# Later layers' attention heads in pairs, keys by queries, weights summed by GpSimd

## The reference

```python
def window_gqa(q, k, v, kc, vc, sink):            # 4 heads, 2 of keys; |query - key| <= 128, + context, + sink
    p = softmax([s_loc, s_ctx, s_sink])
    return p_loc @ v_band + p_ctx @ vc
def diff_weights(q, k, v, lam):                   # 4 heads, two maps of width 32 each
    p = softmax(q @ k^T * 32 ** -0.5)
    return (p[:, :, 0] - lam * p[:, :, 1]) @ v    # keys: 512 tokens and 256 of context
def neighbourhood_attn(q, k, v, kc, vc, rpb):     # 4 heads, width 64; bias by relative row and column
    p = softmax([q @ k^T * 64 ** -0.5 + bias, q @ kc^T * 64 ** -0.5])
    return p_loc @ v + p_ctx @ vc
def ctx_attn(q, k, v, sink=None):                 # layer 2 only: the context's own queries, 256 keys
```

## Time and profile before

| what | value |
|---|---|
| median of 3 runs | 3963.61 us (3963.18 to 3972.03) |
| profiled execution, its own time | 3965.11 us |
| its span | 3963.4 us |
| busy: TensorE, VectorE, ScalarE, GpSimd | 3588.4, 1845.8, 1207.2, 1069.6 us |
| mean granted TensorE clock | 0.937 of full speed |

### The profile page before, as it was taken

How to read it: one execution, slowest core, us unless ns; L and a number is a source line. 1 busy time by engine, 2 the same in 40 slices (tenths; PEclk the granted TensorE clock), 3 DMA queues, 4 the chain that set the end, 5 groups by cost and what they waited for, 6 DMA issues and landing times. The chain is left out here.

```text
span 3963.4 us, 46334 instructions
## 1 busy us (share of the span) xinstructions
PE 3588.4 (91%) x17668; PEld 2809.5 (71%) x17668; DVE 1845.8 (47%) x3445; ACT 1207.2 (30%) x1687; POOL 1069.6 (27%) x643
## 2 busy tenths in 40 slices
PE   6997999999687799999989878999999989879998
PEld 5864788878376678885666546888898467557887
DVE  5433433365444465653527773744355417652111
ACT  2253322233311332222015453222344014443222
POOL 2322434444344233441000003343401000024444
PEclk8998999999798899999989878999999998789999
DMA  5510344422000034441110001444454110002221
GB/s 221 203 54 18 121 161 163 154 87 100 26 1 1 30 115 156 160 152 55 54 53 1 1 1 53 154 145 176 147 172 151 64 64 1 1 34 84 101 89 65
DMA packets 54942, 355.62 MB, mean 90 GB/s; under 512 B 5888, under 2 KB 6912, under 8 KB 19456
## 3 DMA queue, kind: packets, MB, share of 16 engines
q1 hardware_dynamic: 54496, 351.35, 24.4%
q10 hardware_dynamic: 288, 2.10, 0.1%
HBM read 351.33 MB, written 2.10 MB: 89 GB/s over the span
## 5 line engine op out<-in xcount | busy, mean ns | idle before, releaser
L382 POOL TENSOR_TENSOR W_LO<-ring,W_HI 128x2048 fp32r<-128x2048 f32 (+1 forms) x177 | 729.5, 4121 | 1092.2 <-ACT W_HI L370 1092.2
L438 PE MATMUL PS<-H_HI,W_HI 128*128 128x512 f32 (+1 forms) x1888 | 715.0, 379 | 29.9 <-DVE H_LO L817 23.8
L439 PE MATMUL PS<-H_LO,W_HI 128*128 128x512 f32 (+1 forms) x1888 | 704.6, 373 | 0.0
L440 PE MATMUL PS<-H_HI,W_LO 128*128 128x512 f32 (+1 forms) x1888 | 704.4, 373 | 0.0
L370 ACT ACTIVATE W_HI<-ring 128x2048 fp32r<-128x2048 f32 (+1 forms) x214 | 366.2, 1711 | 480.5 <-PE PS L428 442.9
L438 PEld LDWEIGHTS PS<-H_HI,W_HI 128*128 128x128 f32 x1888 | 360.4, 191 | 94.5 <-issue 32.9
L440 PEld LDWEIGHTS PS<-H_HI,W_LO 128*128 128x128 f32 x1888 | 360.0, 191 | 63.2
L439 PEld LDWEIGHTS PS<-H_LO,W_HI 128*128 128x128 f32 x1888 | 360.8, 191 | 59.5 <-issue 0.2
L859 DVE SCALAR_TENSOR_TENSOR PS<-ring,SC,PS 128x256 f32<-128x256 f32 x768 | 376.3, 490 | 27.0
L426 PE MATMUL PS<-HID_HI,W_HI 128*128 128x512 f32 (+1 forms) x880 | 325.6, 370 | 4.8 <-DVE W_LO L382 4.0
L527 POOL TENSOR_TENSOR W_LO<-ring,W_HI 128x512 fp32r<-128x512 f32 x16 | 23.2, 1454 | 1121.0 <-ACT W_HI L517 1120.7
(11 more groups left out here) (309 smaller groups left out, 5582.0 us busy)
## 6 DMA issues: line engine op xcount, KB each, us to landing
ring<-w_tiles SPq DMA_DIRECT2D x273, 1024.0 KB, 4.8
ring<-d_tiles SPq DMA_DIRECT2D x80, 704.0 KB, 4.1
X<-xT SPq DMA_DIRECT2D x1, 2048.0 KB, 12.6
WORK<-rope_tables ACTq DMA_DIRECT2D x2, 1024.0 KB, 7.5
outT<-H SPq DMA_DIRECT2D x8, 256.0 KB, 2.2
CN<-consts SPq DMA_DIRECT2D x1, 1379.0 KB, 16.3
X<-ctxT SPq DMA_DIRECT2D x1, 1024.0 KB, 9.6
PR<-params SPq DMA_DIRECT2D x1, 465.5 KB, 3.3
```

The source lines that it names most:

```text
L382: eng.tensor_tensor(W_LO[:, b, 0:w], ring[:, g % SLOTS, 0:w], W_HI[:, b, 0:w].bitcast(F32), ALU.subtract).then_inc(sig("tile_split"), 1)
L438: pe.matmul(to, hi[:, cols(k, j)], x_hi(k), start=k == 0, stop=False)
L439: pe.matmul(to, hi[:, cols(k, j)], x_lo(k), start=False, stop=False)
L440: mm = pe.matmul(to, lo[:, cols(k, j)], x_hi(k), start=False, stop=k == n - 1)
```

## The change

1. Layers 2 and 3 take the keys-by-queries form. `mixer_tasks` makes for each layer eight main tasks over 512 queries: window heads in pairs (0, 3) and (1, 2), seven steps (two context tiles, the sink, four key tiles of 256 or 384 queries with masks); neighbourhood heads in pairs, six steps, four with a bias; two-map heads in pairs for map 0 and then map 1, six steps. Each has six maxima products. Layer 2 adds a context task of one or two steps behind each. The stage is one, without the barrier in its middle.
2. The sums: instead of a ones-product per step, GpSimd adds the weight tiles of a task up (`TILE_SUMS`, two sets in turn), and TensorE sums over keys by one product per task (`totals`) into the bank of the maxima; also in layer 0.
3. Heads of successive tasks go to two banks in turn (`heads_at`), in place of one bank.
4. `pair_order` spreads the maxima evenly (`wanted`): as many per step as are needed for the next task's start.
5. The neighbourhood bias, now wanted with keys on partitions, is transposed once per layer (`pe_bias_turned`, `act_bias_turned`) into `BT_TURNED`, behind all of `dve_bias`.
6. The scale of 0.125 goes into the copies of the queries (`act_copy_tiles`, one call split in two); a ScalarE chained copy of one element stands between Ln and Exp.

```diff
@@ pair_order
+            def wanted(g):
+                n = 0
+                for k in range(at, len(q_items)):
+                    left = first[q_items[k][1]] - g
+                    if left > 0:
+                        n = max(n, -(-(k + 1 - at) // left))
+                return n
...
                     order.append(("scores", p, steps[g][1]))
-                    order += next_maxima(p)
-                    at += len(next_maxima(p))
+                    n = wanted(g)
+                    if n and may_come(at, p):
+                        order.append(q_items[at])
+                        at, n = at + 1, n - 1
...
+                while g < len(steps) and n > 0 and may_come(at, p):
+                    order.append(q_items[at])
+                    at, n = at + 1, n - 1
+                for q in closing.get(g, []):
+                    order += [("totals", q, 0), ("heads", q, 0)]
@@ pe_pairs
+        def heads_at(p):
+            return 3072 + (p % 2) * 512
...
-                if x == 0:
-                    before = p if task["own_banks"] is None else p - task["own_banks"]
-                    if before:
-                        pe.wait_ge(sig("pair_heads_done"), b_h + before)
+                if x == 0 and p >= 2:
+                    pe.wait_ge(sig("pair_heads_done"), b_h + p - 1)
...
-                    for u, unit in enumerate(task["units"]):
-                        f = unit["off"]
-                        k = slice(0, P if c is not None else 1)
-                        mm = pe.matmul(PS[f:f + 64, task["t_at"] + q0:task["t_at"] + q1], ones[k, 0:64],
-                                       weight_tile(tasks, g, u)[k, o:o + q1 - q0],
-                                       start=first and task["own_banks"] is None, stop=end, skip_group_check=True)
...
+            def totals(p):
+                task = tasks[p]
+                w = task["tiles"] * P
+                wait_maxima_bank(("totals", p, 0))
+                x = len(task["steps"]) - 1
+                pe.wait_ge(sig("pair_tiles_added"), b_a + 2 * added[p, x] + 2)
+                a = maxima_bank(0)
+                for u, unit in enumerate(task["units"]):
+                    f = unit["off"]
+                    mm = pe.matmul(PS[f:f + 64, a:a + w], ones[:, 0:64], TILE_SUMS[p % 2][u][:, 0:w], start=True, stop=True)
+                mm.then_inc(sig("pair_totals_ready"), 1)
@@ act_pairs
+            def totals(p):
+                w = tasks[p]["tiles"] * P
+                if p:
+                    act.wait_ge(sig("pair_heads_done"), b_h + p)
+                act.wait_ge(sig("pair_totals_ready"), b_t + p + 1)
+                act.activation(SCALES[:, 0:w], PS[:, maxima_bank(0):maxima_bank(0) + w], ACT.Ln).then_inc(sig("pair_maxima_read"), 1)
+                chain(act.activation(SM[:, 46:47], SM[:, 1:2], ACT.Copy))
                 act.activation(SCALES[:, 0:w], SCALES[:, 0:w], ACT.Exp, scale=-1.0).then_inc(sig("pair_scales_ready"), 1)
@@ pool_pairs
+                if len(s["parts"]) == 2:
+                    w = q1 - q0
+                    return pool.tensor_tensor(total[:, 0:w], tile[:, 0:w], tile[:, w:2 * w], ALU.add)
+                if x == 1 and len(tasks[p]["steps"][0]["parts"]) == 1:
+                    before = weight_tile(tasks, g - 1, u)
+                    if q0:
+                        pool.tensor_copy(total[:, 0:q0], before[:, 0:q0])
+                else:
+                    before = total
+                return pool.tensor_tensor(total[lanes, q0:q1], before[lanes, q0:q1], tile[lanes, o:o + q1 - q0], ALU.add)
@@ the turned bias
+        def pe_bias_turned(pe):
+            pe.wait_ge(sig("bias_masked"), base("pe", "bias_masked", 1) + 1)
+            for h in range(4):
+                for j in range(7):
+                    o = h * 1024 + j * P
+                    mm = pe.transpose(PS[:, o:o + P], BT[:, h, 12 - 2 * j:14 - 2 * j, :].rearrange("p s c -> p (s c)"), ident)
+                mm.then_inc(sig("bias_turned"), 1)
@@ mixer_tasks
+            for heads in ((0, 3), (1, 2)):
+                q_steps, steps = [], [plain_step(4, 0, T), plain_step(5, 0, T), dict(parts=[(None, 0, T, 0)], masks=(), bias=None)]
+                for i in range(NT):
+                    lo, hi = max(i - 1, 0), min(i + 1, NT - 1)
...
+                    steps.append(plain_step(i, lo * P, (hi + 1) * P, masks))
+                both([window_unit(h) for h in heads], 1.0, q_steps + context_steps(), steps, [window_out(h) for h in heads])
+            for n in range(2):
...
+                    q_steps.append(dict(products=[(i, 0, T, 0)], reads=[(0, 1, T, 0, i, bias)]))
+                    turned = lambda u, i=i, n=n: BT_TURNED[:, 2 * n + u, (3 - i) * P:(7 - i) * P]
+                    steps.append(plain_step(i, 0, T, bias=turned))
...
+            for n in range(2):
+                for m in range(2):
+                    q_steps = [dict(products=[(i, 0, T, 0)], reads=[(0, 1, T, 0, i, None)]) for i in range(NT)]
+                    steps = [plain_step(c, 0, T) for c in range(6)]
+                    both([diff_unit(2 * n + u, m) for u in range(2)], 32 ** -0.5, q_steps + context_steps(), steps,
+                         [(slice(0, P), H[:, 4 + n, :])], minus=SM[:, 42:43] if m else None)
```

440 lines of the change are left out of this document (158 added, 282 removed).

## The result

| what | before | after |
|---|---|---|
| median, same chip | 3965.23 us (3963.18 to 3972.03, 4 runs) | 3901.64 us (3896.79 to 3905.92, 4 runs) |
| ratio, 95% interval | | 0.9837 (0.9821 to 0.9853) |
| profiled execution, span | 3965.11, 3963.4 us | 3896.79, 3895.0 us |
| mean granted clock | 0.937 | 0.948 |

The change is faster by 63.6 us where 85.5 were forecast: inside the range, 23.6 above the predicted time. The profiled executions differ by 68.3, so 17 of the 23.6 can be looked up stage by stage. Of the rest, 4.9 is that the profiled execution is the quickest of its four, and 1.5 that the forecast counts from 3963.6 and the profiled execution before took 3965.1.

A forecast was written before the change was run, and what follows sets the result against it. The prediction had attention's two-map part at VectorE's pace, TensorE waiting for its weights. Gains 47.5 + 40, less 16 for bias, plus 8 for table loads and 6 for layer 0, took 3963.6 to 3878 us, range 3845 to 3935.

The forecast's parts named there:

- layer 0: Layer 0's pairs: ones-products and waits for heads gone, totals and a longer tail new; about -6 us, between 0 and -10.
- layer 2's stage: Layer 2's attention: lead-in 20, products 182, clock 6, waits 40, tail 5, so 253 us for 293, gain 40.
- layer 3's stage: Layer 3's attention: lead-in 20, products 149, clock 6, waits 13, tail 4, so 192 us for 239.5, gain 47.5.
- turned bias, two layers: Bias stages of layers 2 and 3: 28 transposes about 6.5 us and a last copy with waits, +8 per layer.
- table loads, two layers: Normalization after the stage: four loads of 1.283 us become none, three on ScalarE's path, -4 us per layer.
- TensorE's prices: Stage bodies: layer 0's product prices at full clock, two heads at once, give 149 us in layer 3, 182 in layer 2.
- The lead-in: Start of layers 2 and 3's stages, up to the first scores: nothing to hide behind, 20 us per layer.
- The clock: Start of each stage body: low clock for 12.7 us as in layer 0, half of that lost, 6 us per layer.
- The dips rival: Two-map tasks of layers 2 and 3: clock dips to 0.73, +66 us less 15 of hidden waits, 3929; chance 0.12.
- The waits in the body: TensorE's waits, mainly for the one bank of maxima: 13 us in layer 3, 40 in layer 2.
- the rival's price for 1.9: GpSimd becomes the bound: an add costing 1.9 us, not 1.385, lengthens four window tasks by 7 each, 3906; chance 0.09.
- VectorE and GpSimd block each other: Attention stages: every 128x512 VectorE operation costs 1.6 us whatever its operands, slower at 4020; chance 0.05.

The follow-up runs named there:

- e12: e11 with each maximum coming as soon as it may, as in e3, in place of evenly spread: 3917.84 us, 0.9872 of the kernel before.
- e4: Changed kernel plus surplus products behind the first task's maxima products in each layer's lead-in: 3892.51 us, 0.9808 of the kernel before.
- e8: Changed kernel with every task's heads in one bank, totals and heads in the step of its last outputs: 3922.51 us, 0.9865 of the kernel before.
- e7: Changed kernel plus a surplus GpSimd copy of the sum behind each of its additions: 3920.93 us, 0.9901 of the kernel before.
- e2: Kernel before with the new helpers (GpSimd adds, two heads banks, spread maxima) in layer 0's pairs only: 3960.13 us, 0.9981 of the kernel before.
- e3: Changed kernel with each maximum as soon as it may come, up to two tasks ahead, not evenly spread: 3977.01 us, 1.0021 of the kernel before.
- e1: Changed kernel's pairs with the old helpers (ones-products every step, one heads bank, maxima as soon as possible): 4022.01 us, 1.0127 of the kernel before.
- e10: e9 plus e4's surplus products in the three lead-ins: 3881.35 us, 0.9778 of the kernel before.
- e11: e10 plus one surplus product per task, just ahead of the transpose of the maxima: 3872.33 us, 0.9758 of the kernel before.
- e9: Changed kernel with one heads bank as in e8, the freed bank holding the totals: 3900.71 us, 0.9821 of the kernel before.
- e6: Changed kernel with layer 2's eight context tasks all behind its eight full tasks: 3908.89 us, 0.9851 of the kernel before.

## Why the prediction was right, and where it was not

| term | forecast | profile |
|---|---|---|
| layer 0 | -6 | -3.9 |
| layer 2's stage | -40 | -29.9 |
| layer 3's stage | -47.5 | -40.4 |
| turned bias, two layers | +16 | +13.2 |
| table loads, two layers | -8 | -7.2 |
| sum | -85.5 | -68.2 |

- **What bounds it**: right. VectorE is off the path, TensorE sets the pace, pairs of 32 rows do overlap: L1173 with 32x512, x4, takes 1.13 us, as with 64 rows.
- **TensorE's prices**: right to 2% in the sum, partly by luck. Layer 2's body is busy 196.4 us, and without half of its 34.5 us at half clock 179 (forecast 182); layer 3's 156.7 less 9.4 is 147 (149). The forecast adds score and maximum products one behind the other; in the two-map tasks they run partly at once (e12), which saved some of the 12.7 us of overlap in layer 3. Without it the prices are some 4% short, by an estimate from e12: its body has next to no overlap and is busy 180 us; less 17 by halves and 8 of surplus it is 155 for 149.
- **The lead-in**: 20 forecast, 20.3 measured, twice. It was priced at half clock, and e4 shows that this is what it hangs on.
- **The clock**: the term that was mis-sized most, "half of that is lost again: 6 per layer". It took layer 0's 12.7 us for the start, where 4.9 and 8.7 were measured, and no dips after it, where 29.5 and 10.2 were. By halves the clock costs 17 in layer 2 and 9 in layer 3, 14 more than forecast, of 17 us by which the two stages are over. Part of it lies in waits: by busy time, products and clock together are over by 8 and 2. The sign "clock 1.00 after the first 33 us" didn't come true. The dips rival had the mechanism but put it in the wrong place, all two-map tasks at 0.73. They come in pieces anywhere; layer 3's two-map tasks ran at 1.00 throughout in the profiled execution. That dips differ between executions is seen in their mean clocks (e8).
- **The waits in the body**: 45 (with the tail) against 46.2 in layer 2, 17 against 22.0 in layer 3. The mechanism, the shared bank, was right; left out was the transpose that waits for the last maximum to be combined (L1181 <- L1299, 8.3 us in layer 3).
- **GpSimd**: hidden, as forecast; its addition measured 1.29, not 1.385, and the rival's price for 1.9 came out at 19 to 25 for 28, though mostly at the ends of stages and not in window tasks (e7).
- **VectorE and GpSimd block each other**: out, 0.68 to 0.69 for every form with an operand in PSUM.
- **Turned bias**: its transposes ran at 0.19 to 0.20 us each, 5.4 and 5.7 us for 28, not 6.5, and its stages became 6.5 and 6.7 us longer, not 8. **Table loads**: none in the normalization, 3.9 and 3.3 us gone for 4.
- **Layer 0**: 3.9 in the profile, 7.5 by e2's many executions, for 6.

What wasn't forecast at all is how much rests on the even spread: the maxima's order is worth 75 us (e3) and the helpers together 120 (e1), more than the whole gain.

## What to carry to other kernels

When TensorE is the bound and waits often and briefly, price its products at the full clock and then look at the granted clock by windows, in several executions: the same program came out 25 us apart (e8), and a reordering that adds no work cost 75, most of it by the clock (e3). Where TensorE must wait for another engine's read, a surplus product into a bank that is free costs little in the wait and may keep the clock up (e4, e10, e11); at half clock it can be longer than the wait (layer 0 in e4). When heads fill only half of the rows, put products of the other half beside them (e12). And judge a move to a slower engine by what it takes from the bound, and look for its backlog at the end of the stage (e7).

## What the runs showed of the hardware

- Two groups of executions 25 us apart came from one program on one core (e8), with mean granted clocks of 0.948 to 0.949 and 0.938 to 0.940; e1's six fall apart in the same way. e9 with fewer waits had the median of the changed kernel, and by the ratio 6 us less.
- Against the changed kernel, a us at half clock went with 0.26 to 0.58 us of stage (e6 layer 2: 10.3 for 39; e8: 27.5 for 68; e3 layer 3: 63 for 110), but waits and overlap changed too. By TensorE's busy time it was 0.41 in e8, 0.46 in e6 and 0.47 in e9 (layer 2: 28.0, 17.9 and 24.9 us), where 0.5 would be a TensorE that never waits.
- Products on different strips of 32 rows ran at once across two tasks: six products in 1.50 us up to the next outputs, against 2.31 one group behind the other (e12).
- VectorE's 128x512 operations with one operand in PSUM kept 0.68 to 0.69 us beside GpSimd's additions.
- TensorE stayed at 1.2 GHz for 35 us with no idle time in the trace (e3, 3445 to 3480). The Trainium skill (TensorE: Matmul & The Clock Gate, HAM oscillation — how this bites in real kernels) has the clock fall in gaps in which TensorE waits. The waits before the dip at 2272 and the filled waits of e11 go with it, though no wait ahead of that dip was over 1.4 us and the page's are longer ones, for DMA; that it stays low with TensorE busy throughout isn't what that rule leads one to expect, and here the measurement decides. What in the products of a two-map task kept it low in e3, and not in the changed kernel, stays open.
